# First projections of the mixers in rounded pieces, three one-pass products in place of one float32 product, and a new order of stages

## The reference, cut to what matters

```
proj = h @ w_in          # 1024 x 2840
(q, k_c, v_c, k_s, v_s, k_w, v_w, gl, conv_in, rq, rk, rv, rg) = split(proj)
o_a = nsa_mixer(q, k_c, v_c, k_s, v_s, k_w, v_w, gl, ...)   # compressed, selected and window attention
o_b = conformer_conv(conv_in, ...)                          # gate, 31-tap convolution, norm, pointwise
o_c = retention(rq, rk, rv, rg, ...)
x = x + concat[o_a, o_b, o_c] @ w_out
```

## Time and profile before

| | |
|---|---|
| time, median of 3 runs | 1304.18 us (1302.77 to 1304.25) |
| span of the profiled execution | 1302.2 us |
| mean granted TensorE clock | 0.993 |
| mixer of layer 0 in the span | 11.2 to about 173 us |
| mixer of layer 1 in the span | 361.7 to about 522 us |

### The profile page before, as it was taken

How to read it: one execution, slowest core, us unless ns; L and a number is a source line. 1 busy time by engine, 2 the same in 40 slices (tenths; PEclk the granted TensorE clock), 3 DMA queues, 4 the chain that set the end, 5 groups by cost and what they waited for, 6 DMA issues and landing times.

```text
span 1302.2 us, 15655 instructions
## 1 busy us (share of the span) xinstructions
PE 1275.3 (98%) x6043; PEld 1022.5 (79%) x6043; DVE 965.1 (74%) x1090; ACT 819.7 (63%) x1195; POOL 31.5 (2%) x21
## 2 busy tenths in 40 slices
PE   8999999999999999999999999999999999999996
PEld 6867568888888675788888888888888888888885
DVE  2476364455424764898899989989899899889897
ACT  2125354444411353687888888888888878878885
POOL 0000000000000000010000000000000000000300
PEclk9999999999999999999999999999999999999999
DMA  8206286441520261899999999999999999999981
GB/s 339 114 1 244 94 342 239 185 180 64 216 106 29 93 246 38 359 397 390 376 367 387 385 381 364 390 383 366 399 373 370 393 379 356 389 370 362 413 365 46
DMA packets 35647, 367.58 MB, mean 282 GB/s; under 512 B 4080, under 2 KB 4208, under 8 KB 8048
## 3 DMA queue, kind: packets, MB, share of 16 engines
q1 hardware_dynamic: 32832, 356.56, 69.4%
q0 software_dynamic: 1440, 5.24, 1.0%
q10 hardware_dynamic: 1296, 4.72, 0.9%
HBM read 360.73 MB, written 5.77 MB: 281 GB/s over the span
## 4 chain that ended last, share of the span: by engine, by line
PE 92%; DVE 4%; ACT 2%; issue 1%; DMA 1%; SPq 0%; ACTq 0%; DVEq 0%
PE ps L613 88%; PE ps L616 4%; DVE wlU L1733 1%; DMA ring<-mix_in 1%; ACT arena L1187 1%; DVE arena L1572 0%; DVE wlD L1740 0%; ACT L1234 0%; DVE xn L1975 0%; ACT whU L1279 0%; DVE hTl L1854 0%; DVE arena L1586 0%; DVE x L1704 0%; DVE arena L1669 0%; ACT xn L1125 0%
## 5 line engine op out<-in xcount | busy, mean ns | idle before, releaser
L1733 DVE TENSOR_TENSOR wlU<-ring,whU 128x2048 fp32r<-128x2048 f32 x198 | 453.5, 2291 | 64.3 <-ACT whU L1279 59.6
L1279 ACT ACTIVATE whU<-ring 128x1024 fp32r<-128x1024 f32 x396 | 417.7, 1061 | 60.7 <-PE ps L613 53.2
L613 PE MATMUL ps<-whU,hTh 128*128 128x512 f32 x880 | 352.9, 401 | 1.7 <-DVE wlU L1733 1.7
L613 PE MATMUL ps<-whU,hTl 128*128 128x512 f32 x880 | 345.0, 392 | 0.0
L613 PE MATMUL ps<-wlU,hTh 128*128 128x512 f32 x880 | 343.0, 390 | 0.0
L1740 DVE TENSOR_TENSOR wlD<-ring,whD 128x2048 fp32r<-128x2048 f32 x97 | 222.3, 2291 | 39.2 <-ACT whD L1291 39.0
L1291 ACT ACTIVATE whD<-ring 128x1024 fp32r<-128x1024 f32 x194 | 205.1, 1065 | 59.2 <-PE ps L613 52.8
L613 PEld LDWEIGHTS ps<-whU,hTl 128*128 128x128 f32 x880 | 165.1, 188 | 36.1
L613 PEld LDWEIGHTS ps<-whU,hTh 128*128 128x128 f32 x880 | 165.3, 188 | 33.9 <-DVE wlU L1733 2.5
L613 PEld LDWEIGHTS ps<-wlU,hTh 128*128 128x128 f32 x880 | 166.0, 189 | 32.4
L613 PE MATMUL ps<-whD,gTh 128*128 128x512 f32 x428 | 168.7, 394 | 0.5 <-DVE gTl L1758 0.4
(11 more groups left out here) (217 smaller groups left out, 940.4 us busy)
## 6 DMA issues: line engine op xcount, KB each, us to landing
ring<-moe_in SPq DMA_DIRECT2D x88, 2048.0 KB, 8.4
ring<-moe_in SPq DMA_DIRECT2D x88, 1024.0 KB, 8.6
ring<-ffn_in SPq DMA_DIRECT2D x11, 2048.0 KB, 8.4
ring<-mix_in SPq DMA_DIRECT2D x6, 3072.0 KB, 10.8
ring<-ffn_in SPq DMA_DIRECT2D x11, 1024.0 KB, 6.3
ring<-mix_in SPq DMA_DIRECT2D x4, 2048.0 KB, 13.2
ring<-mix_in SPq DMA_DIRECT2D x2, 2176.0 KB, 8.4
ring<-mix_in SPq DMA_DIRECT2D x2, 2112.0 KB, 13.8
```

What stands on the lines that cost most here:

```text
L613: return nc.tensor.matmul(o, lhsT, rhs, start=first, stop=last, skip_group_check=True)
L1279: A(whU[:, p, :], ring[:, f.slot(J), p * PIECE:(p + 1) * PIECE], ACT.Copy).then_inc(s_hi, 1)
L1733: V.tensor_tensor(wlU[:, w, :], raw, whU[:, w, :].bitcast(F32), ALU.subtract).then_inc(s_lo, 1)
```

## The change

Of each layer's projections all but `vsw` and `rvg` go over to three one-pass products. Their weights, 8 pieces of 1024 by 256, are split on the chip: in stage `piece` n ScalarE writes the rounded part of the piece to one of four homes in memory, and VectorE writes the remainder over the weights in `ring`. In stage `split` k the two engines do the same with the half of `hT` of `nT` k. TensorE waits for the remainder of a piece before it reads the piece. The new stages stand in `HEAD`, whose `conv` parts are spread in another way; `score` 1 goes ahead of `kcv` 1. In the second half, `convB`, `hidT` 0, `hidT` 1 and `rsilu` go ahead of `score` 8, `retcat` ahead of `score` 10, and `rroot` and `retnorm` 1 from `BESIDE[5]` and `BESIDE[6]` to `BESIDE[7]`.

```diff
-HEAD = [("stat", 0), ("nT", 0), ("stat", 1), ("vsw", 0), ("nT", 1), ("rqk", 0), ("vsw", 1), ("rqk", 1),
-        ("cg", 0), ("ca", 0)] + conv(0, 1) + [("q", 0), ("retT", 0)] + conv(1, 4) + [("q", 1), ("retT", 1)] + conv(4, 7) + \
-       [("ks", 0)] + conv(7, 9) + [("kcv", 0), ("score", 0), ("kcv", 1)] + conv(9, 11) + [("score", 1)] + conv(11, 12)
+HEAD = [("stat", 0), ("nT", 0), ("stat", 1), ("split", 0), ("vsw", 0), ("nT", 1), ("piece", 0), ("split", 1),
+        ("piece", 1), ("rqk", 0), ("vsw", 1), ("piece", 2), ("rqk", 1), ("piece", 3), ("cg", 0), ("ca", 0), ("piece", 4)] + \
+       conv(0, 1) + [("piece", 5), ("q", 0), ("retT", 0)] + conv(1, 3) + [("piece", 6), ("q", 1), ("retT", 1)] + conv(3, 5) + \
+       [("piece", 7), ("ks", 0)] + conv(5, 9) + [("kcv", 0), ("score", 0), ("score", 1), ("kcv", 1)] + conv(9, 12)
+
+AHEAD = {6: [("convB", 0), ("hidT", 0), ("hidT", 1), ("rsilu", 0)], 8: [("retcat", 0)]}
...
-          3: [("reto", 0), ("convT", 0)], 4: [("hid", 0), ("cnorm", 0), ("croot", 0)], 5: [("hid", 1), ("cnorm", 1), ("retnorm", 0), ("rroot", 0)],
-          6: [("convB", 0), ("hidT", 0), ("hidT", 1), ("rsilu", 0), ("retnorm", 1)], 7: [("cmpkv", 0), ("conv_pw", 0)],
-          8: [("retcat", 0), ("cscore", 0), ("out", 0)], 9: [("out", 1)],
+          3: [("reto", 0), ("convT", 0)], 4: [("hid", 0), ("cnorm", 0), ("croot", 0)], 5: [("hid", 1), ("cnorm", 1), ("retnorm", 0)],
+          6: [], 7: [("rroot", 0), ("cmpkv", 0), ("conv_pw", 0), ("retnorm", 1)],
+          8: [("cscore", 0), ("out", 0)], 9: [("out", 1)],
...
-                for z in [("probT", k)] + [("score", k + 2)] * (k + 2 < len(UNITS)) + BESIDE[k] + [("pv", k)]] + TAIL
+                for z in [("probT", k)] + AHEAD.get(k, []) + [("score", k + 2)] * (k + 2 < len(UNITS)) + BESIDE[k] + [("pv", k)]] + TAIL
...
+SPLITS = ((VW, 536, 280, "rqk", 1), (RET, 768, 0, "rqk", 1), (CONV, 768, 512, "cg", 0), (CONV, 768, 256, "ca", 0),
+          (QK, 768, 0, "q", 0), (QK, 768, 256, "q", 1), (QK, 768, 512, "ks", 0), (CONV, 768, 0, "kcv", 0))
+RQK_K, RQK_Q, CG, CA, Q0, Q1, KS, KCV = range(8)
+HOMES = 4
...
-            def width_major(o, l, m, col):
-
-                w = weights(l, m, 768)
+            def split_ready(l, n):
+
+                pe.wait_ge(s_mlo, len(SPLITS) * l + n + 1)
+
+            def width_major(o, l, n, half):
+
+                w = slice(half * P, (half + 1) * P)
+                low = piece_of(ringl, l, n)
                 for k in range(KD):
-                    last = mm(o, w[:, k, col:col + P], hT[:, k, :], k == 0, k == KD - 1)
+                    last = three(o, whM[n % HOMES][:, k, w], low[:, k, w], hTh[:, k, :], hTl[:, k, :], k == 0, k == KD - 1)
+                return last
...
+                        pe.wait_ge(s_mhTl, NT * l + k + 1)
+                        split_ready(l, RQK_K)
+                        split_major(o[:, 256:512], l, RQK_K, k)
+                        split_ready(l, RQK_Q)
+                        is_full(split_major(o[:, 0:256], l, RQK_Q, k), l, stage, k)
...
+                    elif stage == "split":
+                        t = slice(k * P, (k + 1) * P)
+                        for half in range(2):
+                            freed(act, l, "nT", k, half)
+                            c = slice(4 * half, 4 * half + 4)
+                            last = A(hTh[:, c, t], hT[:, c, t], ACT.Copy)
+                        last.then_inc(s_mhT, 1)
+                    elif stage == "piece":
+                        m, width, col, reader, at = SPLITS[k]
+                        n = mix_load(l, m)
+                        act.wait_ge(slot_full[n % SLOTS], filled(n))
...
+                        if k >= HOMES:
+                            full(act, l, SPLITS[k - HOMES][3], SPLITS[k - HOMES][4])
+                        elif k == 1:
+                            full(act, l, "nT", NT - 1, 1)
+                        A(whM[k % HOMES][:], piece_of(ring, l, k), ACT.Copy).then_inc(s_mhi, 1)
...
+                    elif stage == "piece":
+                        dve.wait_ge(s_mhi, len(SPLITS) * l + k + 1)
+                        V.tensor_tensor(piece_of(ringl, l, k), piece_of(ring, l, k), whM[k % HOMES][:].bitcast(F32),
+                                        ALU.subtract).then_inc(s_mlo, 1)
```

More of the change, by code:

```diff
@@ L267, in hybrid_trunk_kernel @@
         arena = sb("arena", [P, ARENA])
+        mix_at = {}
         def arena_of(start, end):
@@ L375, in hybrid_trunk_kernel @@
         xl = nc.alloc_sbuf_tensor_at("xl", [P, NT, D], F32R, offset=xn_at)
+        home_at = (arena_at + 4 * 6144, xn_at, arena_at + 4 * mix_at["catT"], arena_at + 4 * (-(-mix_at["cln"] // 8) * 8))
+        whM = [nc.alloc_sbuf_tensor_at(f"whM{h}", [P, KD, FC], F32R, offset=home_at[h]) for h in range(HOMES)]
         beforeb = sb("beforeb", [P, P], BF16)
@@ L449, in hybrid_trunk_kernel @@
         s_warm = sem("s_warm")
+        s_mhT = sem("s_mhT")
+        s_mhTl = sem("s_mhTl")
+        s_mhi = sem("s_mhi")
+        s_mlo = sem("s_mlo")
         s_gather = sem("s_gather")
@@ L630, in weights, with split_major @@
                 return item(l, m)[:, 0:KD * width].rearrange("p (k n) -> p k n", k=KD)
-            def width_major(o, l, m, col):
-                w = weights(l, m, 768)
-                for k in range(KD):
-                    last = mm(o, w[:, k, col:col + P], hT[:, k, :], k == 0, k == KD - 1)
+            def split_ready(l, n):
[3 more added lines that the diff above has]
+                low = piece_of(ringl, l, n)
+                for k in range(KD):
+                    last = three(o, whM[n % HOMES][:, k, w], low[:, k, w], hTh[:, k, :], hTl[:, k, :], k == 0, k == KD - 1)
+                return last
+            def split_major(o, l, n, i):
+                low = piece_of(ringl, l, n)
+                t = slice(i * P, (i + 1) * P)
+                for k in range(KD):
+                    last = three(o, hTh[:, k, t], hTl[:, k, t], whM[n % HOMES][:, k, :], low[:, k, :], k == 0, k == KD - 1)
                 return last
@@ L687, in mixer @@
                         o = begin(l, stage, k)
[L688 to L691, removed]
+                        split_ready(l, Q0 + k)
+                        width_major(o[:, 0:T], l, Q0 + k, 0)
+                        is_full(width_major(o[:, T:2 * T], l, Q0 + k, 1), l, stage, k)
                     elif stage == "ks":
                         o = begin(l, stage)
-                        width_major(o[:, 0:T], l, QK, 4 * P)
-                        is_full(width_major(o[:, T:2 * T], l, QK, 5 * P), l, stage)
+                        split_ready(l, KS)
+                        width_major(o[:, 0:T], l, KS, 0)
+                        is_full(width_major(o[:, T:2 * T], l, KS, 1), l, stage)
                     elif stage == "kcv":
@@ L698, in mixer @@
                             begin(l, stage)
-                        last = width_major(bank(l, stage)[:, k * T:(k + 1) * T], l, CONV, k * P)
+                            split_ready(l, KCV)
+                        last = width_major(bank(l, stage)[:, k * T:(k + 1) * T], l, KCV, k)
                         if k:
@@ L703, in mixer @@
                         o = begin(l, stage)
[L704 to L708, removed]
+                        n = CG if stage == "cg" else CA
+                        split_ready(l, n)
+                        width_major(o[:, 0:T], l, n, 0)
+                        is_full(width_major(o[:, T:2 * T], l, n, 1), l, stage)
                     elif stage == "vsw":
@@ L1534, in mixer @@
                                 .then_inc(s_fold, 1)
+                    elif stage == "split":
+                        dve.wait_ge(s_mhT, NT * l + k + 1)
+                        t = slice(k * P, (k + 1) * P)
+                        for half in range(2):
+                            c = slice(4 * half, 4 * half + 4)
+                            last = V.tensor_tensor(hTl[:, c, t], hT[:, c, t], hTh[:, c, t].bitcast(F32), ALU.subtract)
+                        last.then_inc(s_mhTl, 1)
+                    elif stage == "piece":
+                        dve.wait_ge(s_mhi, len(SPLITS) * l + k + 1)
+                        V.tensor_tensor(piece_of(ringl, l, k), piece_of(ring, l, k), whM[k % HOMES][:].bitcast(F32),
+                                        ALU.subtract).then_inc(s_mlo, 1)
                     elif stage == "ks":
```

17 lines of the change are left out of this document (11 added, 6 removed).

## The result

The changed kernel took 1310.9 us (median of 4 runs, 1309.36 to 1311.59) against 1304.22 (4 runs, 1302.77 to 1305.86): a ratio of 1.0053, 95% interval 1.0039 to 1.0068. It is slower by 0.5%, and the forecast of 1311 was met. The span of the profiled execution is 1309.6 us, 7.4 more than before.

The account below looks back on a forecast made before the run. TensorE, busy 98% of the span, was taken as the bound. Per layer -6.9 products, +4.6 +3.3 +3.1 waits, -0.7 -1.8 moved stages gave +1.6; clock +1.8 made +3.4, +7 in all: 1311 us, range 1300 to 1319.

Parts of the forecast that it names:

- one-pass products: Eight projection stages' worth per layer: a stage falls from 6.91 to 6.05 us, 6.9 less on TensorE per layer.
- clock: Falls behind `rqk` 0, `q` 0, `probT` 0 at 0.9 each, -0.9 at `out` 0: +1.8 us per layer, between -1.8 and +4.1.
- new waits: TensorE idles per layer: 4.1 us at `rqk` 0, 3.3 at `q` 0, 3.1 at `probT` 0, 1.2 at `retcat`.
- waits gone: Per layer, 0.74 us ahead of `pv` 0 and 3.0 at `pv` 6, `cmpkv` and `out` 0 go.
- the 0.126 of the gather: Price of a one-pass product of 256 columns, from 32 in a row in the earlier trace; three make 0.377 us.
- my bounds: Price of a one-pass product of 256 columns: 0.114 us below, 0.15 above.
- the 0.119: Product price from which down the faster rival decides if the clock does as before; faster rival's chance 0.17.
- The 0.22 us per layer for each 0.001 us: Faster rival: what each 0.001 us in the price of a one-pass product is worth per layer; chance 0.17.
- 0.5 behind it: Behind the wait at `rqk` 0: piece 1's remainder ready at 374.1, first 24 products ended at 373.5, 0.5 us more wait.
- the near tie of the two chains: At `q` 0: load of QK with its copy done at 399.6, just before VectorE is free.
- The 1.8 that the earlier trace show for one fall: At `out` 0 in the kernel before: 5.37 us at clock 0.55 against 3.60 of `out` 1, 1.8 lost.
- my account: At `probT` 0: VectorE does eight taps to 430.1 ahead of the maximum of `score` 0; TensorE idles 3.1 us.

Follow-up runs that it names:

- two candidates: Changed kernel with no neighbours sharing a stationary operand, 1310.39 us; changed kernel with `q` 0 and `q` 1 products alternating halves of the bank, 1310.42 us.
- The runs with products of zeros: Changed kernel with 30, 28 and 28 bfloat16 products of zeros ahead of `rqk` 0, `q` 0, `probT` 0: median 1305.48 us of 12 runs.
- one swap: Changed kernel with `vsw` 1 ahead of `rqk` 0: 1300.89 us, ratio to the kernel before 0.9989.
- The last run but one: Changed kernel with `vsw` 1 first, pieces ahead, `kcv` piece split before that of `q` 0, `rvg` 0 ahead of `q` 0, taps respread: 1290.59 us, ratio 0.9912.
- the run with the moves alone: Kernel before with only the moved stages of the second half, projections and `HEAD` as before: 1299.95 us, ratio 0.9979.

## Why the prediction was right

The forecast held, and in part by luck: two of its terms were off by about 6 us each, in opposite ways. The mechanism was right: cheaper products, the waits where they were said to be, released as said, and the clock behind them. Over both layers, us:

| term | forecast | measured |
|---|---|---|
| one-pass products | -13.8 | -20.0 |
| new waits (`rqk` 0, `q` 0, `probT` 0, `retcat`) | +24.4 | +26.1 |
| waits gone | -7.4 | -8.0 |
| clock | +3.6 | +10.3 |
| sum | +6.8 | +8.4 (span: +7.4) |

**Products.** I took the 0.126 of the gather; the trace has 0.118, 5.66 a stage against 6.91, 1.25 saved eight times. That is inside my bounds and just below the 0.119 from which the prediction had the time fall under that of before if the clock did as before. By the table, products and waits alone make -1.9 us, less than timing can tell; the clock decided between no change and a slowdown. The 0.22 us per layer for each 0.001 us stands in the prediction without its working. By the count of 384 products it is 0.38 of TensorE's work, and the rest must go into longer waits; the waits did measure 1.7 more than forecast. The Trainium skill (FP8 and Floating Point Precision, TensorE Precision Notes) states the four passes of true float32; that reduced precision takes one was my reading of it. The trace has 0.118 against 0.432, a ratio of 3.7. Why the gather pays 0.126 stays open: two candidates were tried and changed nothing.

**Split.** ScalarE's copy of 2048 took 1.91 (estimated 1.92), VectorE's subtraction 2.29, layout no matter. Both costs lay beside TensorE's work but for the three waits.

**Waits.** `rqk` 0: 3.90 for 4.1, and no 0.5 behind it, since at half speed the first 24 products hid piece 1. `q` 0: 3.31 and 3.99 for 3.3. In layer 1 ScalarE waited for the load of QK until 403.02, and its copy ended just as VectorE came free of `ca` at 404.89: the near tie of the two chains that the prediction had. In layer 0 the load was the later one, VectorE waited 0.82 for the copy, and this is the 0.7 that the forecast lacks. `probT` 0: 3.62 and 3.61 for 3.1. `retcat`: 1.90 for 1.2, mis-sized in both layers. The waits at `pv` 0, `pv` 6, `cmpkv` and `out` 0 went as said.

**Clock.** This term was mis-sized. I gave each fall a chance and a price by 16 products at half speed, and so 0.9 us. All three came in both layers, cost 1.7 or 3.4 each, and the one at `out` 0 went wholly. The 1.8 that the earlier trace rows show for one fall would have been the nearer price. The runs with products of zeros tie 11.4 us of span to the falls. The Trainium skill (TensorE: Matmul & The Clock Gate, Why this matters for your kernels) has idle gaps between bursts put the engine back to its lower clock; behind the three new waits the rule held six times in six in the changed kernel's profiled execution, and following it would have sized the term better. The runs show that it isn't strict: with `vsw` 1 first, 3.20 and 3.31 us of idle before `q` 0 (layers 0 and 1) were followed by 1.00.

**What the experiments add.** The cause of the slowdown is shown for `rqk` 0: one swap gave back 10 us. For `probT` 0 my account (eight taps ahead of the maximum) was only half of it: with the taps deferred in one block the wait moved on to `pv` 1; with VectorE's gaps shortened and the deferred taps in blocks of at most 7.3 us it went. The last run but one speaks for the gaps, since there more taps stood ahead of the maximum, but it also put `rvg` 0 there: how much is the gaps' and how much the blocks', no run separates.

## What to carry over

Cheaper products on the bounding engine move the bound to the queues that feed them: read, ahead of the first wait, where the feeding engine itself is idle and for what, close those gaps first. If its work must be deferred, look at what stands behind it in the same queue: here a block of 12.8 us opened a new wait and blocks of at most 7.3 us did not. That the block's length alone decides is not shown. A wait that is put into a stretch without gaps costs its length and then, here, mostly 1.7 to 3.4 us of clock. A term priced from another place in the kernel carries an error times its count: 0.008 us a product was 6 us.

## What the runs showed of the hardware

In the first 600 us of all 14 traces, each stretch below full clock cost close to 1.7, 3.4 or 5.1 us (in the changed kernel 1.7 in six places and 3.4 in two, up to 538 us). The same program falls in some executions and not in others: the run with the moves alone spanned 1295.0 at a mean clock of 0.996 and 1303.2 at 0.990. A fall can also follow an idle of only 1.9 us where small products stand on both sides: in that run, behind `retcat`, 36 small products took 5.31 us against the 2.92 in the changed kernel behind the same wait. And a longer one need not bring a fall: the 3.20 and 3.31 us before `q` 0 above.
